# The third up unit of each MLP's middle chunks as seven products of half contraction, half features and half tokens

## The reference, cut to what matters

```python
D_MODEL, SEQ, D_FF = 1024, 512, 4 * 1024

def sq_relu_mlp(h, w_up, w_down):
    return jnp.square(jax.nn.relu(h @ w_up)) @ w_down

# in each of the two layers of second_block, after the mixer (attention, then a short convolution):
f = sq_relu_mlp(rmsnorm_2(x, g[2]), w_mlp_up[i], w_mlp_down[i])
x = x + rmsnorm_2(f, g[3])
gate = jax.nn.sigmoid(rmsnorm_2(x, g[4]) @ w_ple_gate[i])
e = (p[i] @ w_ple_proj[i]) * gate
x = x + rmsnorm_2(e, g[5])
```

## Time and profile before

| | |
|---|---|
| median of 3 runs | 1714.99 us (1714.67 to 1715.71) |
| the profiled execution | 1714.86 us |
| its span in the profile | 1713.1 us, 24293 instructions |
| PE matmuls | 1693.0 us busy, 9087 instructions |
| DVE | 1198.9 us (70%) |
| ACT | 918.6 us (54%) |
| POOL | 169.8 us (10%) |
| DMA | 160.68 MB, mean 94 GB/s |
| granted TensorE clock | 0.998 |

### The profile page before, as it was taken

The page is one execution under the profiler, slowest core; times in us unless marked ns, Lnnn a source line. Parts: engine busy times, 40 slices in busy tenths (PEclk is TensorE's granted clock), DMA queues, the critical chain, the costliest instruction groups (busy, mean ns, idle before and its releaser), DMA issues.

```text
span 1713.1 us, 24293 instructions
## 1 busy us (share of the span) xinstructions
PE 1693.0 (99%) x9087; PEld 1449.8 (85%) x9087; DVE 1198.9 (70%) x1848; ACT 918.6 (54%) x1545; POOL 169.8 (10%) x147
## 2 busy tenths in 40 slices
PE   9999999999999999999999999999999999999998
PEld 7888877888788897789898988878887999898977
DVE  6378877776567777576586976785566848587866
ACT  4267875665436667466545364642235746354555
POOL 2011212000300000220000002420003000000041
PEclk9999999999999999999999999999999999999999
DMA  8222124214242222223241423313322232323321
GB/s 268 85 74 74 40 74 101 74 50 147 74 112 75 74 75 81 74 74 128 71 147 68 130 74 111 110 56 109 107 86 74 99 123 75 123 76 122 111 74 50
DMA packets 151053, 160.68 MB, mean 94 GB/s; under 512 B 18089, under 2 KB 126150, under 8 KB 150694
## 3 DMA queue, kind: packets, MB, share of 16 engines
q1 hardware_dynamic: 150790, 159.22, 29.6%
q10 hardware_dynamic: 160, 0.07, 0.0%
HBM read 150.43 MB, written 4.19 MB: 90 GB/s over the span
## 4 chain that ended last, share of the span: by engine, by line
PE 95%; DVE 2%; ACT 2%; issue 0%; DVEq 0%; ACTq 0%
PE bank L1053 29%; PE bank L1054 29%; PE bank L1055 29%; PE bank L1402 2%; PE bank L1426 1%; PE bank L1321 1%; PE bank L1310 1%; DVE act_a L2485 0%; PE bank L1696 0%; ACT act_a L1793 0%; DVE work L2516 0%; PE bank L1236 0%; PE bank L1220 0%; PE bank L1345 0%; PE bank L1252 0%
## 5 line engine op out<-in xcount | busy, mean ns | idle before, releaser
L1053 PE MATMUL bank<-act_a,split_weights 128*128 128x512 f32 (+1 forms) x1392 | 547.7, 393 | 6.2 <-DVE act_a L2483 2.0
L1055 PE MATMUL bank<-act_a,split_weights 128*128 128x512 f32 (+1 forms) x1392 | 541.1, 389 | 0.0
L1054 PE MATMUL bank<-act_a,split_weights 128*128 128x512 f32 (+1 forms) x1392 | 540.5, 388 | 0.0
L1053 PEld LDWEIGHTS bank<-act_a,split_weights 128*128 128x128 f32 x1392 | 261.6, 188 | 62.9 <-issue 6.0
L1055 PEld LDWEIGHTS bank<-act_a,split_weights 128*128 128x128 f32 x1392 | 261.3, 188 | 55.4
L1054 PEld LDWEIGHTS bank<-act_a,split_weights 128*128 128x128 f32 x1392 | 261.7, 188 | 50.2 <-issue 0.2
L2425 DVE TENSOR_TENSOR split_weights<-raw_weights,split_weights 128x2048 fp32r<-128x2048 f32 x67 | 154.6, 2307 | 147.9 <-ACT split_weights L1738 134.9
L1738 ACT ACTIVATE split_weights<-raw_weights 128x2048 fp32r<-128x2048 f32 x63 | 120.3, 1909 | 199.3 <-PE bank L1055 199.2
L1053 PE MATMUL bank<-act_b,split_weights 128*128 128x256 f32 (+1 forms) x648 | 207.1, 320 | 0.0
L1055 PE MATMUL bank<-act_b,split_weights 128*128 128x256 f32 (+1 forms) x648 | 206.4, 319 | 0.0
L1054 PE MATMUL bank<-act_b,split_weights 128*128 128x256 f32 (+1 forms) x648 | 206.3, 318 | 0.0
(11 more groups left out here) (326 smaller groups left out, 2948.3 us busy)
## 6 DMA issues: line engine op xcount, KB each, us to landing
raw_weights<-in_w_mlp_up SPq DMA_DIRECT2D x32, 1024.0 KB, 5.4
raw_weights<-in_w_mlp_down SPq DMA_DIRECT2D x32, 1024.0 KB, 4.9
raw_weights<-in_w_in SPq DMA_DIRECT2D x18, 1024.0 KB, 5.2
raw_weights<-in_w_conv_in SPq DMA_DIRECT2D x12, 1024.0 KB, 5.1
raw_weights<-in_w_attn_in SPq DMA_DIRECT2D x16, 512.0 KB, 5.4
raw_weights<-in_w_ple_gate SPq DMA_DIRECT2D x8, 1024.0 KB, 4.7
raw_weights<-in_w_out SPq DMA_DIRECT2D x4, 1024.0 KB, 4.9
raw_weights<-in_w_attn_in SPq DMA_DIRECT2D x4, 1024.0 KB, 5.3
```

Source lines behind the costliest of these rows:

```text
L1053: nc.tensor.matmul(dst, w[0], a[0], start=first, stop=False)
L1054: nc.tensor.matmul(dst, w[0], a[1], start=False, stop=False)
L1055: mm = nc.tensor.matmul(dst, w[1], a[0], start=False, stop=last)
```

## The change

In chunks 1 and 2 of both MLPs (four times in all) the third up unit (u = 2) is no longer plain but goes in seven products too: halves of the contraction, the unit's two tiles of 128 features, and halves of the tokens. Product i of 84 / 7 = 12 matmuls over 256 tokens goes to half a PSUM bank, two products to a bank, four banks for the unit (`UP_HOME`). ScalarE copies the first product out (`o`), VectorE combines the seven in four steps into `sq` (`d8` to `d11`), and relu and square read from there.

What comes with it:

- **Banks.** `UP_BANKS` gives the up units of chunks 1 and 2 the banks (0, 1), (2, 3), (4, 5, 6, 7), (0, 1). `up_bank_read` says which read PE waits for before it writes a bank: the first product of down unit 0 (bank 0) now waits for the relu of up unit 3.
- **Ring.** The third unit takes seven blocks, and the fourth is aligned to four again, 48 blocks for the chunk in place of 44. `block_freed` works out what frees a block.
- **Weights.** `G2` and `F2` (DVE) make the sums of the third unit's weights, `g14` to `g20` the high and low parts of its seven operands; `N6`, `N7` split the fourth unit in halves, where `U2` and `U3` split the third and the fourth whole.
- **Input sums.** The normed input is needed as sums t1 to t4 of its blocks (contraction by tokens), for four kp: `X` scales two tiles by the gain (ACT, into `sq`), `Q` makes the four sums (DVE), `H` their high (ACT) and low (DVE) parts. Steps 0 and 1 lie in chunk 0's down phase, 2 and 3 at the start of chunk 1. Made once per MLP, used in both middle chunks.
- **Room.** The sums lie where the residual x, the embedding part and the split p lay. These go to DRAM on ScalarE's queue ahead of chunk 0 (`keep_outside`, 2 + 1 + 1 MB) and come back at the start of chunk 3 (`bring_back`, `B0`); the residual's addition and the embedding's projection wait for it.
- Some semaphores are merged (`mixed`, `kept_added`, `pad_zero`).

```diff
+PRODUCT_UPS = ((), (2,), (2,), ())
...
-        return 2 if j < 4 else 4 if (c, j) == (LAST, 7) else 0
+        return 2 if j < 4 and j not in PRODUCT_UPS[c] else 4 if (c, j) == (LAST, 7) else 0
...
-    return name.startswith("mlp") and u % 8 >= 4 and u < 8 * LAST + 6
+    return name.startswith("mlp") and (u % 8 in PRODUCT_UPS[u // 8] or u % 8 >= 4 and u < 8 * LAST + 6)
+UP_WIDTHS = [[4 if u in PRODUCT_UPS[c] else 2 for u in range(4)] for c in range(MLP_CHUNKS)]
+UP_BANKS = [[[(sum(widths[:u]) + g) % 8 for g in range(widths[u])] for u in range(4)] for widths in UP_WIDTHS]
...
+        def up_bank_read(layer, c, b, before=4):
+            for u in reversed(range(before)):
+                if b in UP_BANKS[c][u]:
+                    return up_read(layer, c, u, UP_BANKS[c][u].index(b))
+            if b < PRODUCTS:
+                return product_read(layer, c - 1, 1, b)
...
+        UP_OPERAND = ("b11", "b21", "t2", "t1", "t3", "b22", "t4")
+        UP_HOME = ((0, 0), (1, 0), (1, 1), (2, 0), (2, 1), (3, 0), (3, 1))
...
+        ACT_THIRD = ("s0 b0 t0 g14 g15 v0 g16 g17 s1 b1 g18 t1 g19 v1 g20 o2 N6 N7 p0 p1 p2 p3 s2 b2 t2 v2 "
+                     "p4 p5 p6 p7 s3 b3 p8 t3 p9 v3 p10 p11 p12 p13 ")
+        ACT_MLP = ("s0 b0 t0 v0 " + ACT_PLAIN + "p14 p15 a0 p16 a1 p17 a2 p18 X0 a3 p19 a4 H0 p20 a5 p21 a6 X1 p22 p23 p24 H1 p25 p26 "
+                   "p27 a7 n0 a8 a9 n1 a10 n2 a11 a12 a13 n3",
+                   "X2 H2 X3 H3 " + ACT_THIRD + "p14 p15 p16 p17 p18 p19 p20 p21 p22 p23 p24 p25 p26 p27 n0 n1 n2 n3",
...
+        DVE_THIRD = ("T0 b0 y0 t0 g14 g15 v0 g16 g17 F2 T1 b1 g18 y1 t1 g19 v1 g20 d8 N6 d9 d10 N7 S0 p0 d11 p1 p2 z0 p3 "
+                     "T2 b2 y2 t2 v2 p4 p5 p6 S1 p7 T3 b3 y3 p8 t3 p9 v3 z1 p10 p11 p12 p13 ")
+        DVE_MLP = (DVE_PLAIN + "S2 p14 p15 p16 z2 p17 p18 p19 Q0 p20 H0 S3 p21 p22 Q1 p23 z3 p24 p25 H1 p26 p27 n0 n1 n2 n3",
+                   "Q2 H2 Q3 H3 G2 " + DVE_THIRD + DVE_DOWN + "n0 a7 a8 n1 a9 a10 n2 a11 a12 n3 a13",
...
+            def mlp_up_products(layer, name, c, u):
+                pl = Place(tab, name, 8 * c + u)
+                number = product_unit_number(layer, c, u)
+                for i in range(PRODUCTS):
+                    if i < PRODUCTS - 1:
+                        pe.wait_ge(prod_split, (PRODUCTS - 1) * number + i + 1)
+                    else:
+                        pe.wait_ge(w_split, pl.u + 1)
+                    if UP_OPERAND[i][0] == "t":
+                        pe.wait_ge(x_sum_ready, x_sum_count(layer, KT // 2 - 1, 7, 7))
+                    g, half = UP_HOME[i]
+                    if half == 0:
+                        pe.wait_ge(*up_bank_read(layer, c, UP_BANKS[c][u][g], before=u))
+                    w = [product_weights(pl, i, hl) for hl in (0, 1)]
+                    for kp in range(KT // 2):
+                        three(mlp_bank(name, UP_BANKS[c][u][g])[:, TOKENS[half]], [w[hl][:, kp * P:kp * P + P] for hl in (0, 1)],
+                              [up_operand(UP_OPERAND[i], hl, kp) for hl in (0, 1)], half == kp == 0,
+                              kp == KT // 2 - 1 and (half == 1 or g == 0), prod_done if kp == KT // 2 - 1 else None)
...
             def mlp_products(layer, name, c, d):
...
                     elif part == 0 and c:
-                        pe.wait_ge(tile_read, up_tile + i + 1)
+                        pe.wait_ge(*up_bank_read(layer, c, i))
...
+                def keep_outside():
+                    act.wait_ge(x_ready, n["x"])
+                    nc.scalar.dma_start(x_stash, x_tiles).then_inc(stash_saved, 16)
+                    act.wait_ge(tile_read, tab.extra[name] + 4)
+                    nc.scalar.dma_start(e_stash, e_tiles).then_inc(stash_saved, 16)
+                    nc.scalar.dma_start(p_stash, p_parts).then_inc(stash_saved, 16)
...
+                def up_mix(c, u, step):
+                    number = product_up_number(layer, c, u)
+                    second, third, fourth = (mlp_bank(name, b) for b in UP_BANKS[c][u][1:])
+                    if step == 0:
...
+                        dve.wait_ge(*up_copied(layer, c, u))
+                        dve.wait_ge(prod_done, product_done(layer, c, u, 2))
+                        V.tensor_tensor(in_halves(sq[:, 0, :]), in_halves(second[:, :]), first, ALU.add).then_inc(up_mixed, 1)
+                        return
+                    dve.wait_ge(up_mixed, 4 * number + step)
+                    if step == 1:
+                        dve.wait_ge(prod_done, product_done(layer, c, u, 4))
+                        V.tensor_tensor(in_halves(sq[:, 1, :]), in_halves(third[:, :]), both, ALU.add).then_inc(up_mixed, 1)
+                    elif step == 2:
+                        V.tensor_tensor(sq[:, 0, TOKENS[1]], third[:, TOKENS[0]], sq[:, 1, TOKENS[1]], ALU.add).then_inc(up_mixed, 1)
+                    else:
+                        dve.wait_ge(prod_done, product_done(layer, c, u, 6))
+                        V.tensor_tensor(sq[:, 1, :], fourth[:, :], sq[:, 1, :], ALU.add).then_inc(up_mixed, 1)
```

More of the change, by code:

```diff
@@ new lines, in relu_done, with up_read @@
+        def relu_done(layer, number):
+            c, u = [(b, w) for b in range(MLP_CHUNKS) for w in PRODUCT_UPS[b]][number % UP_PER_LAYER]
+            return squares_made(number // UP_PER_LAYER, c, u) + 2
+        def up_read(layer, c, u, g):
+            if u not in PRODUCT_UPS[c]:
+                return tile_read, tab.tile[tab.first[f"mlp{layer}"] + 8 * c + u] + g + 1
+            number = product_up_number(layer, c, u)
+            return up_copied(layer, c, u) if g == 0 else (up_mixed, 4 * number + (0, 1, 3, 4)[g])
@@ new lines, in up_bank_read, with x_sum @@
+        def up_bank_read(layer, c, b, before=4):
[4 more added lines that the diff above has]
+                return product_read(layer, c - 1, 1, b)
+            if c == 1:
+                return tile_read, tab.tile[tab.first[f"mlp{layer}"] + 8]
+            return up_bank_read(layer, c - 1, b)
+        def x_sum(what, hl, kp):
+            if what == "t4":
+                return head_qk[:, 2 * hl + kp // 2, TOKENS[kp % 2]]
+            home = e_sums[:, kp, :] if what == "t3" else x_sums[:, kp + (KT // 2 if what == "t2" else 0), :]
+            return home[:, TOKENS[hl]]
@@ L655, in up_unit_number @@
             return 4 * MLP_CHUNKS * layer + 4 * c + u
[L657 to L677, removed]
+        ACT_PLAIN = "U3 s1 b1 t1 v1 p0 p1 p2 p3 s2 b2 t2 v2 p4 p5 p6 p7 s3 b3 p8 t3 p9 v3 p10 p11 p12 p13 "
@@ L1561, in mlp_up @@
                 pe.wait_ge(w_split, pl.u + 1)
-                tiles = [2 * u + m for m in range(2)]
-                dst = [mlp_bank(name, t) if c else bank(pl, m) for m, t in enumerate(tiles)]
+                dst = [mlp_bank(name, UP_BANKS[c][u][m]) if c else bank(pl, m) for m in range(2)]
                 for k in range(KT):
-                    for m, t in enumerate(tiles):
+                    for m in range(2):
                         if k == 0 and c == 0:
                             empty(pl.tile, m)
-                        elif k == 0 and t < PRODUCTS:
-                            pe.wait_ge(*product_read(layer, c - 1, 1, t))
                         elif k == 0:
-                            pe.wait_ge(tile_read, tab.tile[tab.first[name] + 8 * c])
+                            pe.wait_ge(*up_bank_read(layer, c, UP_BANKS[c][u][m], before=u))
                         at = k * 256 + m * P
@@ new lines, in x_sums_lo @@
+                def x_sums_lo(kp):
+                    both = x_sums[:, kp:KT:KT // 2, :]
+                    dve.wait_ge(x_sum_hi, x_sum_count(layer, kp, 5, 3))
+                    low(both[:, :, TOKENS[1]], x_first_sums(kp), both[:, :, TOKENS[0]], x_sum_ready)
+                    for at, what in enumerate(("t3", "t4")):
+                        dve.wait_ge(x_sum_hi, x_sum_count(layer, kp, 5, 4 + at))
+                        low(x_sum(what, 1, kp), x_sum_made(what, kp), x_sum(what, 0, kp), x_sum_ready)
@@ L3136, in mix @@
                     dst, a, b, after = MIXES[k]
-                    mixed = far_mixed if o else near_mixed
                     if k == 0:
```

286 lines of the change are left out of this document (216 added, 70 removed).

## The result

The changed kernel takes 1735.01 us (median of 4 runs, 1734.08 to 1736.34) against 1714.87 us before (4 runs, 1714.67 to 1715.71): a ratio of 1.0117 with a 95% interval of 1.01 to 1.0135, +20.1 us. The forecast was 1730.0, +15.1 us: direction and place right, 5 us short. The profiled execution took 1734.21 us with a span of 1732.4 us, 19.3 more than before.

What follows compares the result with a forecast made beforehand. PE's instruction stream was taken as the bound, busy 1693.0 of 1713.1 us. Matmul gain -0.85, weight wait +1.6 and bank wait +3.03 gave +3.78 us, four times +15.1: 1730.0 us, range 1721 to 1738.

Steps and rivals of the forecast that it cites:

- Term A: Third up unit of chunks 1 and 2 in seven products: 10.03 us in place of 10.88, 0.85 us gained each time.
- Term C: First down product waits for bank 0 until ScalarE's relu, behind four copies, has read it: 3.03 us per chunk.
- Term B: Fourth up unit waits for its weights, split in halves late in VectorE's queue: 1.6 us per chunk, bounds 0.7 to 3.
- The zeros: Input sums, DRAM stores and loads, merged semaphores and zeroed padding: hidden, no time added.
- chunk 0's margin: Input sums added in chunk 0's down phase stay hidden with 1.2 us left at the tightest; 1 us per MLP if late.
- Rival 4: Preparation in chunk 0 and at chunk 1's start also late, 1 to 2 us per MLP: 1733 us, 10%.
- The sum: Chunks 1 and 2 of both MLPs: -0.85 + 1.6 + 3.03 = +3.78 us each, four times +15.1 us.
- The clock: PE's clock stays up after the 3.03 us wait before the down phase; a fall would give 1735 to 1746 us.
- rival 3: Clock falls in the longer wait before the down phase, two products run at the lower clock: 1740 us, 8%.
- The signs of being wrong: First down product right behind the fourth unit, the four gaps absent, or matmuls after them over 0.119 us apart.

Runs made afterwards that it cites:

- the banks moved: Changed kernel with the fourth up unit of chunks 1 and 2 writing banks 2 and 3 in place of 0 and 1: 1719.06 us, ratio 1.0022.
- the relu moved: Changed kernel with the fourth unit's relu and square (s3) ahead of copies p4 to p7 on ScalarE, banks as changed: 1721.28 us, ratio 1.0035.
- the kernel before with only its banks wrapped: Kernel before, all up units plain, with the fourth up unit of chunks 1 and 2 writing banks 0 and 1: 1732.76 us, ratio 1.0096.
- The version with nothing but Term A: Changed kernel with banks 2 and 3, N6 and N7 ahead of d8, s3 between p5 and p6, S1 ahead of p6 on VectorE: 1711.77 us.
- the three edits together: Changed kernel with banks 2 and 3 for the fourth unit, its relu ahead of p4 to p7, N6 and N7 ahead of d8 to d10: 1717.2 us.
- the halves first: Changed kernel with the fourth unit's halves N6 and N7 ahead of d8, d9 and d10 on VectorE: 1730.56 us, ratio 1.0093.
- the matmuls in the wait: Changed kernel with 22 unused 256-token matmuls into bank 7 ahead of the first down product's wait in chunks 1 and 2: 1730.11 us, ratio 1.0082.
- banks and halves: Changed kernel with banks 2 and 3 for the fourth up unit, N6 and N7 ahead of d8 to d10, p4 to p7 still ahead of s3: 1714.56 us.

## Why the prediction was right in kind and 5 us short

- **Term A**, -0.85: the third unit takes 10.00 us, the up phase without waits 42.68: -0.85. Right.
- **Term C**, +3.03: the start of the first down product is 3.30 us behind the start before it, where 0.22 is the normal distance, so 3.08. ScalarE's 0.26 + 2.10 + relu + 0.14 came as summed, and VectorE held nothing up, as argued. Right; shown by the banks moved, the relu moved, and the kernel before with only its banks wrapped.
- **Term B**, +1.6: measured 11.35 - 10.00 = 1.35, and 0.11 more at the second matmul behind the wait (0.34 us behind the first, where 0.23 is normal). The queue of VectorE was as listed: with E = 1422.36 here, N7 ends at E + 11.3 in place of E + 11.6. ScalarE began the pair of relus 0.2 us earlier than taken, and from T1 to the end of N7 it took 9.43 us in place of 9.52. Right within its bounds.
- **The zeros** (input sums, DMAs, semaphores, chunk 0's margin) were zeros: chunk 0 and chunk 3 didn't move. Rival 4 fell.
- **The sum** per middle chunk, +3.78: measured -0.85 + 1.35 + 0.11 + 3.08 = 3.69 by its terms, +3.68 by the windows.
- **The clock** is the term that failed. It had 0 in the sum and stood as rival 3 with 8%, because the wait of 2.03 us up to 666.54 left the clock at 1.00. That was too little to rest on. The row ends at 666.00, before PE goes on, and the falls in these runs mostly begin behind that point. It was one execution: in four others the same wait of 2.03 us was followed by the lower clock (the last section has the rows). And for a wait of 2.9 us it said nothing, while the sentence that C is "longer than the first and comes after dense work" pointed the other way. Three of the four waits cost 1.5 us each, 4.6 us: the near end of rival 3 (one product at the lower clock, 1.3 us), not its middle. The rule cited from the Trainium skill, "TensorE: Matmul & The Clock Gate", section "HAM oscillation — how this bites in real kernels", was the better guide: three of the four waits of 2.9 us went by it, though not "each time". Counting the rival with its one-product price, 4 x 1.3, would have given 1735.2; that this is the measured median to 0.2 us is partly luck, since it counts four falls of 1.3 us where the profile has three of 1.5.
- **The signs of being wrong.** One of the three came true: behind three of the four waits the matmuls start 0.213 us apart and not 0.119. The range held the result because it took in the near end of rival 3, not because of the sum.
- PE's busy time was to be 3 us less and was 2.9 more; without the clock's 4.6 it is 1.7 less, so the forecast's sign failed with the same term. The version with nothing but Term A shows 1689.7, 3.3 less.

## What to carry to other kernels

When a stage takes more PSUM banks, follow the ring to the bank that the next stage writes first, and look who reads it last and what stands ahead of that read in its engine's order. A wait of TensorE near 3 us cost here the wait and, in nine cases of twelve, half as much again for the clock; price both, or keep the engine at work. One execution in which the clock stayed up behind a wait doesn't show that the wait is safe: look at several. Removing a wait by putting one engine's step first holds back what others need from it: the three edits together missed their gain until the relu went between the copies, not ahead of them.

## What the runs showed of the hardware that was not expected

- The clock's fall is not certain for one and the same wait: equal waits of 2.91 us were followed by a slow stretch in three of four cases in the changed kernel (not at 1447.80), in three of four in the wrapped one (not at 855.60), and waits of 3.0 to 3.3 us in three of four with the halves first: there behind the shortest (3.04) and the longest (3.27), but not behind one of 3.24 at 854.46.
- A wait of 2.03 us can be followed by the fall too. The one that ends near 666.5, some 140 us ahead of the first middle chunk, was followed by a granted clock of 0.50 in four of the ten profiled executions (all three together, the wrapped kernel, the matmuls in the wait, banks and halves) and by none in the other six. First all three together, then the kernel before:

```profile
666.22 0.50 PE L1160 MATMUL bank<-act_a,split_weights 128*128 128x512 f32 x1 [2.03 <-DVE act_a L2673]
668.00:669.00 1.00, 1.00 (x6) 1.00 (x5) 0.04 (x1) 0.35 (x1) 0.00 (x0) 0.50 0.00 0
...
668.00:669.00 1.00, 1.00 (x10) 0.96 (x9) 0.36 (x1) 0.43 (x2) 0.00 (x0) 1.00 0.00 0
```

  It cost some 1.6 us: from the end of the wait to the first MLP's chunk 1 it is 143.4 us with the fall (666.22 to 809.59) and 141.7 without (666.54 to 808.28). In the last 21 runs of the kernel before, the granted clock of a run goes from 0.998 (1714.69 to 1715.23 us) to 0.995 (1717.99 us): part of the spread of one and the same kernel goes with the clock. What decides whether a wait brings it down is open; no experiment here separates it.
- In eight of the nine slow stretches at the start of a down phase the fall comes late: the distances grow 0.2 to 1.5 us after PE has started again. In the ninth (wrapped, 1445.23) the clock was down before PE started. They last 12 to 17 matmuls at 0.213 us, then the distance is 0.12 us again at once.
- A matmul over 256 tokens at the 1.2 GHz level starts every 0.213 us, a little less than one over 512 tokens at 2.4 GHz, 0.227.
